# Latent attention: gate units of 256 columns placed between the heads, output projection split by input

## The chip, the cores and the metric

The kernel runs on one core of one Trainium2 chip. The metric is the device time of one execution in microseconds (us), lower being better; the time before is the median of three runs.

## What is computed

Two transformer blocks in float32 for 256 tokens of width 2048: a retention layer, a layer of latent attention, a layer of forgetting and dilated attention, and an expert lookup. The change touches the latent layer alone. Cut to what matters:

```python
def mla_branch(h, pos, w_in, q_norm_g, w_uq, kv_norm_g, w_ukv, w_out):
    cq, ckv, k_rope, g = split(h @ w_in)             # 512, 512, 64, 2048 columns
    q = (rmsnorm(cq, q_norm_g) @ w_uq)               # 16 heads of 128 + 64 (the 64 get rope)
    kv = (rmsnorm(ckv, kv_norm_g) @ w_ukv)           # 16 heads of 128 + 128
    k_rope = rope(k_rope)                            # one, shared by the heads
    o = causal_block_attention(q, k, v)              # softmax per head, 256 x 256
    return (silu(g) * o) @ w_out                     # 2048 x 2048
# and then x = x + gate * y, followed by the block's last rmsnorm
```

## The kernel before, in words

Every large product runs as three float32r matmuls (high by high, high by low, low by high; `three`, L1846 to L1848). The weights come in units of 512 KB. For each unit SP starts a DMA into a ring of eight buffers, ACT writes the rounded high part (`cast`, L696), DVE subtracts it to get the low part (`step`, L1160), and PE runs the unit's matmuls: 24 of 256 columns where the weight is the stationary operand (`unit_T`), 12 of 512 columns where the activation is (`unit_tok`). High and low parts have four buffers, so the cast of unit w+4 waits until PE has used up unit w. Each engine's order of work is written out by hand, one function per engine, and engines meet through counting semaphores; PE's `take(b)` is the wait until PSUM bank b has been read.

The latent layer goes: the two latents (CQ, CKV); the first 512 gate columns (G0), whose Silu (ACT, L847) goes straight from PSUM into `SGM`; the transposes of the normed latents ("C"); the shared key part (KRW), which is turned by a small matmul (`turn_rope`, L2061) and rotated by three DVE operations (`rotate`, L1263, L1265, L1268); the other 1536 gate columns in 24 units (G1, three groups of two banks each); and then the heads in four groups of four. A group has eight units (`lat_group`): 0 and 1 give the queries, 2 and 3 the part to be rotated, 4 and 5 the keys (copied from PSUM by DVE, L1485), 6 and 7 the values (copied by ACT, L882). Group 0 runs ahead of the heads; the units of the next group stand in the second to the fourth step of the group before, so the first step of a group, and the last group, have none. A head is four score matmuls (L2126 to L2129), a maximum on DVE (`soft`, L1280), two exponentials on ACT (`exps`, L743), a division on DVE (L1500), three transposes on PE (`flip`, L2107) and a copy on ACT (L750) one step later, and three matmuls with the values (L2139 to L2141) two steps later; DVE multiplies the result by the Silu in `SGM` (L1506). After the last head ACT and DVE split `SGM` into its high and low parts in four slabs (L902, L1516), and the output projection O2 runs: four column groups of eight units, each followed by a scaling and an addition to X on DVE (L1246, L1249).

In the heads banks 0 and 1 hold queries and then keys, 2 and 3 the rotated part and the values, 4 and 5 scores, 6 the transposes, 7 the head's output.

## Time and profile before

| what | value |
|---|---|
| median of 3 runs | 3264.48 us (3261.02 to 3265.04) |
| the profiled execution's own time | 3269.56 us |
| its span | 3267.8 us |
| PE matmul busy over the span | 2901.9 us (89%) |
| DVE busy | 2159.6 us (66%) |
| ACT busy | 1106.9 us (34%) |
| mean granted PE clock | 0.936 |
| G1's gate units, heads and O2 | from 1057 to 1367 us of the span |

The profile is one execution; its times are counted from the start of its span, which is 1.8 us shorter than the execution. A busy share is an average over stages with different limits. Matmuls are pipelined and their ends are modelled, so PE's pace is read from the distance of starts.

### The profile page before, as it was taken

How to read it: one execution, taken by the hardware profiler on the slowest of the kernel's cores; microseconds unless marked ns; L12 is line 12 of the kernel's file. 1: busy time of each engine (PE TensorE's matmuls, PEld its weight loads, DVE VectorE, ACT ScalarE, POOL GpSimd, SP SyncE). 2: the span in 40 equal slices, each digit the busy share in tenths (PEclk: the TensorE clock that was granted, in tenths of full speed). 3: DMA queues.
4: the chain of work that ended last, by engine and by line, in shares of the span. 5: the costliest groups of instructions: out<-in, count | busy, mean ns of one | idle time of the engine just before them, and what ended most of it. 6: DMA issues, size and time to landing. Idle time of an engine off the chain costs nothing.

```text
span 3267.8 us, 40653 instructions
## 1 busy us (share of the span) xinstructions
PE 2901.9 (89%) x15944; PEld 2427.8 (74%) x15944; DVE 2159.6 (66%) x3196; ACT 1106.9 (34%) x1716; POOL 665.4 (20%) x580
## 2 busy tenths in 40 slices
PE   3689999998989998899999989999997767999980
PEld 3689999996868977699888779888876656555540
DVE  6777777776765445534335556896568999666667
ACT  2133334334444444434334443111026766000000
POOL 5510000000000000000000000324432557544445
PEclk9689999998999999889989889999999898999995
DMA  8777787776866633446333343999994888999997
GB/s 292 245 235 255 249 274 260 261 256 200 289 196 168 176 108 116 149 123 187 104 97 113 122 150 117 353 314 389 407 347 148 279 287 311 393 410 410 410 398 294
DMA packets 359152, 807.95 MB, mean 247 GB/s; under 512 B 40121, under 2 KB 99777, under 8 KB 358193
## 3 DMA queue, kind: packets, MB, share of 16 engines
q1 hardware_dynamic: 284336, 497.89, 45.3%
q0 software_dynamic: 74624, 307.47, 25.5%
q8 instruction: 126, 2.06, 0.2%
q14 instruction: 66, 0.53, 0.0%
HBM read 803.16 MB, written 2.10 MB: 246 GB/s over the span
## 4 chain that ended last, share of the span: by engine, by line
PE 36%; DMA 18%; DVE 12%; POOL 5%; issue 4%; ACT 2%; DVEq 0%; ACTq 0%; POOLq 0%
PE ps L1846 10%; DMA s<-in_up_rows,s 10%; PE ps L1847 10%; PE ps L1848 10%; DMA s<-in_down_rows,s 8%; DVE s L1789 5%; POOL s L681 5%; DVE s L1811 1%; PE ps L2224 1%; DVE s L1754 1%; PE ps L2107 1%; DVE s L1757 1%; PE ps L2226 1%; DVE s L1661 1%; DVE s L1667 1%
## 5 line engine op out<-in xcount | busy, mean ns | idle before, releaser
L1846 PE MATMUL ps<-r,r 128*128 128x256 f32 (+2 forms) x3248 | 1065.1, 328 | 76.7 <-DVE r L1160 44.3
L1847 PE MATMUL ps<-r,r 128*128 128x256 f32 (+2 forms) x3248 | 1046.2, 322 | 0.0
L1848 PE MATMUL ps<-r,r 128*128 128x256 f32 (+2 forms) x3248 | 1045.0, 322 | 0.0
L1160 DVE TENSOR_TENSOR r<-s,r 128x1024 fp32r<-128x1024 f32 (+1 forms) x532 | 648.1, 1224 | 575.9 <-ACT r L696 575.7
L696 ACT CAST r<-s 128x1024 fp32r<-128x1024 f32 (+1 forms) x532 | 550.2, 1039 | 898.5 <-PE ps L1848 851.9
L1846 PEld LDWEIGHTS ps<-r,r 128*128 128x128 f32 x3248 | 641.3, 197 | 134.1 <-DVE r L1160 41.3
L1847 PEld LDWEIGHTS ps<-r,r 128*128 128x128 f32 x3248 | 641.2, 197 | 43.0 <-issue 4.6
L1848 PEld LDWEIGHTS ps<-r,r 128*128 128x128 f32 x3248 | 640.3, 197 | 41.0
L1811 DVE SCALAR_TENSOR_TENSOR s<-s,s,s 128x1152 f32<-128x1152 f32 x256 | 362.6, 1416 | 158.2 <-DMA s<-in_up_rows,s 153.5
L1789 DVE CUSTOM_DVE_ANT_0 s<-s,s 128x1152 f32<-128x1152 f32 x256 | 344.7, 1353 | 110.1 <-DMA s<-in_down_rows,s 109.7
L681 POOL DMA_INDIRECT s<-in_down_rows,s x256 | 273.7, 1069 | 578.2 <-DVE s L1789 370.1
L2342 PE MATMUL ps<-s,s 128*128 128x256 f32 x1792 | 387.2, 379 | 0.0
L2455 PE MATMUL ps<-s,big 128*128 128x448 f32 x1024 | 386.9, 541 | 0.0
L2342 PEld LDWEIGHTS ps<-s,s 128*128 128x128 f32 x1792 | 340.5, 190 | 46.0
L681 POOL DMA_INDIRECT s<-in_up_rows,s x256 | 291.5, 1139 | 246.4 <-DVE s L1811 208.8
L2455 PEld LDWEIGHTS ps<-s,big 128*128 128x128 f32 x1024 | 195.4, 191 | 190.9 <-issue 190.9
L1178 DVE SCALAR_TENSOR_TENSOR s<-s,s,s 128x512 f32<-128x512 f32 x304 | 225.6, 779 | 2.5 <-DMA s<-in_ada_w 1.1
L665 POOL DMA_DIRECT2D s<-in_final_norm_g x1 | 0.6, 618 | 1093.6 <-DVE s L1506 1093.6
L1131 ACT ACTIVATE s<-s 128x1152 f32<-128x1152 f32 x2 | 2.3, 1164 | 469.1 <-DVE s L1811 469.1
L1051 ACT COPY big<-ps 128x512 f32<-128x512 f32 x64 | 39.2, 613 | 344.6 <-PE ps L2342 344.6
L2407 PE MATMUL ps<-s,s 128*128 128x128 f32 x384 | 59.4, 303 | 56.9 <-DVE s L1779 54.6
L2407 PEld LDWEIGHTS ps<-s,s 128*128 128x128 f32 x384 | 51.9, 208 | 73.1 <-issue 54.2
(281 smaller groups left out, 2506.6 us busy)
## 6 DMA issues: line engine op xcount, KB each, us to landing
s<-in_ada_w SPq DMA_DIRECT2D x192, 512.0 KB, 5.4
s<-in_ret_w_in SPq DMA_DIRECT2D x128, 512.0 KB, 5.3
s<-in_down_blocks SPq DMA_DIRECT2D x128, 448.0 KB, 6.6
s<-in_up_blocks SPq DMA_DIRECT2D x128, 448.0 KB, 6.8
s<-in_w_in SPq DMA_DIRECT2D x96, 512.0 KB, 3.8
s<-in_ret_w_in SPq DMA_DIRECT2D x128, 256.0 KB, 4.0
s<-in_ret_w_out SPq DMA_DIRECT2D x64, 512.0 KB, 5.5
s<-in_mla_w_in SPq DMA_DIRECT2D x48, 512.0 KB, 3.7
```

The source lines that it names most:

```text
L681: g.indirect_dma_start(out=row_buf(n), out_offset=None, in_=down_rows if n < 256 else up_rows, in_offset=bass.IndirectOffsetOnAxis(ap=EI[t ...
L696: s.copy(hi_of(w), raw_of(w)).then_inc(*hi_made.to(w))
L1160: v.tensor_tensor(lo_of(w), raw_of(w), hi_of(w).bitcast(F), ALU.subtract).then_inc(*lo_made.to(w))
L1178: r = v.scalar_tensor_tensor(out=acc[h], in0=w, scalar=cact[:, k:k + 1], in1=acc[h], op0=ALU.mult, op1=ALU.add)
L1789: v.tensor_tensor_reduce(row_buf(n), row_buf(n), HNG[:, t, :], 1.0, 0.0, ALU.mult, ALU.add, HD[t][:, j:j + 1]).then_inc(*rows_used.to(n))
L1811: v.scalar_tensor_tensor(out=X[:, t, DCOL:], in0=row_buf(256 + n), scalar=HD[t][:, j:j + 1], in1=X[:, t, DCOL:], op0=ALU.mult, op1=ALU.add ...
L1846: pe.matmul(o, lh, rh, start=start, stop=False, skip_group_check=True)
L1847: pe.matmul(o, lh, rl, start=False, stop=False, skip_group_check=True)
L1848: return pe.matmul(o, ll, rh, start=False, stop=stop, skip_group_check=True)
L2342: r = pe.matmul(bank[4 + q % 4][:, j * 256:(j + 1) * 256], w[:, k, :], XNT[:, k, :], start=k == 0, stop=k == DCOL // 128 - 1)
L2407: r = pe.matmul(bank[b][:, k * 128:(k + 1) * 128], o1[:, k, :], o2[:, k, :], start=True, stop=True)
L2455: r = pe.matmul(bank[2 * t + b][:, 0:HCOL], CO[t][:, i2 // 32, i2 % 32, :], sbuf[i2 % NS][:, b * HCOL:(b + 1) * HCOL], start=i2 == 0, stop ...
```

## The change

The 24 gate units of G1 leave their place ahead of the heads. They become six pieces of 256 gate columns with four units each (`unit(mla_in, u * 512, ..., 256, 4)`: four 128-row blocks of 256 columns where a unit had two of 512), placed after the score matmuls of a head: four units in the first and two in the second head of each group. All six pieces use PSUM bank 3; ACT runs the Silu of a piece when its first unit of the next piece is due. The values move from banks 2 and 3 to banks 0 and 1. The rotation of the shared key part moves behind the first two units of group 0. Three of the four slabs are made in step 14. O2 is split by input: the 16 units that read heads 0 to 7 stand in steps 15 to 17 (`mla_units`), their column groups are scaled and added to X on their own (`mla_add`), and the other 16 follow the last slab. The weights' DMAs follow the new order.

```diff
--- before.py
+++ after.py
-        for g in range(1, 4):
-            cols512(mla_in, 1088 + g * 512)
-        for g in range(4):
-            addw(head_units(uq, g * 768, 192, 0, 128))
-            addw(head_units(uq, g * 768, 192, 128, 64), 512)
-            addw(head_units(ukv, g * 1024, 256, 0, 128))
-            addw(head_units(ukv, g * 1024, 256, 128, 128))
-        for n in range(4):
-            cols512(mla_out, n * 512)
+
+        MLA_GATES = (4, 2, 0, 0) * 4
+        lat_w, gate_w = {}, {}
+
+        def lat_units(g, ks):
+            us = (head_units(uq, g * 768, 192, 0, 128) + head_units(uq, g * 768, 192, 128, 64)
+                  + head_units(ukv, g * 1024, 256, 0, 128) + head_units(ukv, g * 1024, 256, 128, 128))
+            for k in ks:
+                lat_w[g, k] = MG + len(lat_w) + len(gate_w)
+                addw([us[k]], 512 if k in (2, 3) else 1024)
+
+        MG = 282
+        lat_units(0, range(8))
+        for i in range(16):
+            for _ in range(MLA_GATES[i]):
+                j, u = divmod(len(gate_w), 4)
+                gate_w[j, u] = MG + len(lat_w) + len(gate_w)
+                addw([unit(mla_in, u * 512, 1600 + 256 * j, 256, 4)])
+            if i % 4 and i // 4 < 3:
+                lat_units(i // 4 + 1, ((0, 1), (2, 3, 4, 5), (6, 7))[i % 4 - 1])
+        for half in range(2):
+            for n in range(4):
+                addw([unit(mla_out, u * 256, n * 512) for u in range(4 * half, 4 * half + 4)])
...
+        def mla_units(i):
+
+            return {15: range(0, 5), 16: range(5, 10), 17: range(10, 16)}.get(i, ())
...
-            def silu_gate(g):
-                w0 = G0 if g == 0 else G1 + 8 * (g - 1)
-                for u in range(8):
-                    cast(w0 + u + 4)
-                for p in range(2):
-                    s.wait_ge(*(used_up if p else first_bank).at(w0 + 7))
-                    s.activation(flat(SGM[:, 4 * g + 2 * p:4 * g + 2 * p + 2, :]), bank[GATE_BANK[g] + p],
-                                 ACT.Silu).then_inc(*lat_silu.to(2 * g + p))
-
-            silu_gate(0)
...
-            for g in range(1, 4):
-                silu_gate(g)
+
+            def silu_gate(j):
+                s.wait_ge(*used_up.at(gate_w[j, 3]))
+                s.activation(flat(SGM[:, 4 + 2 * j:6 + 2 * j, :]), bank[3], ACT.Silu).then_inc(*lat_silu.to(2 + j))
+
+            def gate_units():
+                for j in range(6):
+                    for u in range(4):
+                        if j and u == 0:
+                            silu_gate(j - 1)
+                        cast(gate_w[j, u] + 4)
+                        yield
...
                 for t in range(2):
-                    s.wait_ge(*(used_up if t else first_bank).at(w0 + 7))
-                    s.copy(VM[a][:, t, :], bank[2 + t]).then_inc(*vm_copied.to((g, t)))
+                    s.wait_ge(*(used_up if t else first_bank).at(lat_w[g, 7]))
+                    s.copy(VM[a][:, t, :], bank[t]).then_inc(*vm_copied.to((g, t)))
...
             for _ in lat_group(0):
                 pass
-            more = None
+            def slab(i):
+                s.wait_ge(*att_out.at(("M", 4 * i + 3)))
+                sl = slice(1024 * i, 1024 * i + 1024)
+                s.copy(flat(OS[0])[:, sl], flat(SGM)[:, sl]).then_inc(*slab_hi.to(("S", i)))
+
+            more, gates = None, gate_units()
             for i in range(18):
                 if i < 16:
                     exps("M", i)
+                    for _ in range(MLA_GATES[i]):
+                        next(gates)
                 if 0 <= i - 1 < 16:
                     flip_copy("M", i - 1)
                 if i % 4 == 1 and i // 4 + 1 < 4:
                     more = lat_group(i // 4 + 1)
                     next(more)
-                elif more is not None and i < 16:
+                elif i % 4 and i // 4 < 3:
                     next(more, None)
                     next(more, None)
-            for i in range(4):
-                s.wait_ge(*att_out.at(("M", 15)))
-                sl = slice(1024 * i, 1024 * i + 1024)
-                s.copy(flat(OS[0])[:, sl], flat(SGM)[:, sl]).then_inc(*slab_hi.to(("S", i)))
-            s.wait_ge(*slab_lo.at(("S", 3)))
-            project_out("O2", O2, 8)
+                if i == 14:
+                    silu_gate(5)
+                    for j in range(3):
+                        slab(j)
+                for u in mla_units(i):
+                    cast(O2 + u + 4)
+            slab(3)
+            project_out("O2", O2 + 16, 4)
...
                         v.wait_ge(*out_read.at((x, n, t)))
+                        if x == "O2":
+                            v.wait_ge(*half_added.at((x, n, t)))
                         v.tensor_tensor(xs, OT[:, t, :], xs, ALU.add).then_inc(*out_added.to((x, n, t)))
...
-            for g in range(1, 4):
-                for u in range(8):
-                    if g == 1 and u == 0:
-                        rotate("KR", 2, 1, KR, cosM, sinM, RAW, RT, None)
-                    step(G1 + 8 * (g - 1) + u)
 
             def lat_group(g):
-                w0, a = MG + 8 * g, g % 2
-                step(w0)
-                step(w0 + 1)
+                a = g % 2
+                step(lat_w[g, 0])
+                step(lat_w[g, 1])
+                if g == 0:
+                    rotate("KR", 2, 1, KR, cosM, sinM, RAW, RT, None)
...
+            def slab(i):
+                sl = slice(1024 * i, 1024 * i + 1024)
+                v.wait_ge(*slab_hi.at(("S", i)))
+                v.tensor_tensor(flat(OS[1])[:, sl], flat(SGM)[:, sl], flat(OS[0])[:, sl].bitcast(F),
+                                ALU.subtract).then_inc(*slab_lo.to(("S", i)))
+
+            def mla_add(n):
+                for t in range(2):
+                    xs, o = X[:, t, n * 512:(n + 1) * 512], at(YG + 4096 + 512 * t, 512)
+                    v.wait_ge(*(used_up if t else first_bank).at(O2 + 4 * n + 3))
+                    if n:
+                        v.wait_ge(*half_added.at(("O2", n - 1, t)))
+                    v.tensor_tensor(o, bank[2 * (n % 2) + t], GBB[:, n * 512:(n + 1) * 512], ALU.mult).then_inc(*steps.to())
+                    v.wait_ge(*steps.at())
+                    v.tensor_tensor(xs, o, xs, ALU.add).then_inc(*half_added.to(("O2", n, t)))
+
+            more, gates = None, (w for _, w in sorted(gate_w.items()))
...
+                    for _ in range(MLA_GATES[i]):
+                        step(next(gates))
...
-            for i in range(4):
-                sl = slice(1024 * i, 1024 * i + 1024)
-                v.wait_ge(*slab_hi.at(("S", i)))
-                v.tensor_tensor(flat(OS[1])[:, sl], flat(SGM)[:, sl], flat(OS[0])[:, sl].bitcast(F),
-                                ALU.subtract).then_inc(*slab_lo.to(("S", i)))
-            v.wait_ge(*slab_lo.at(("S", 3)))
-            project_out("O2", O2, 8, GBB)
+                if i == 14:
+                    for j in range(3):
+                        slab(j)
+                for u in mla_units(i):
+                    step(O2 + u)
+                    if u % 4 == 3:
+                        mla_add(u // 4)
+            slab(3)
+            project_out("O2", O2 + 16, 4, GBB)
...
-            def project_out(x, w0, units, y):
-                        unit_tok(w, u, u == units - 1, b0, y)
+                        unit_tok(w, first + u, u == units - 1, b0, y, None, first)
...
-            def silu_gate(g):
-                w0, b0 = G0 if g == 0 else G1 + 8 * (g - 1), GATE_BANK[g]
-                take(b0)
-                take(b0 + 1)
-                for u in range(8):
-                    unit_T(w0 + u, u, u == 7, b0, HT)
-                    if g == 1 and u == 0:
-                        turn_rope("KR", 2, 256, PMm, RAW)
-                for p in range(2):
-                    free[b0 + p] = lat_silu.at(2 * g + p)
...
-            silu_gate(0)
+            take(4)
+            take(5)
+            for u in range(8):
+                unit_T(G0 + u, u, u == 7, 4, HT)
+            free[4], free[5] = lat_silu.at(0), lat_silu.at(1)
             for p in range(4):
                 turn("C", p, CTOK, lambda t, k: lat_normed.at((k // 4, t)))
             take(2)
             for u in range(2):
                 unit_T(KRW + u, u, u == 1, 2, HT, nk=8, ms=1)
-            for g in range(1, 4):
-                silu_gate(g)
+
+            def gate_units():
+                for j in range(6):
+                    take(3)
+                    for u in range(4):
+                        unit_T(gate_w[j, u], u, u == 3, 3, HT, nk=4, ms=2)
+                        if u == 3:
+                            free[3] = lat_silu.at(2 + j)
+                        yield
 
...
+                if g == 0:
+                    turn_rope("KR", 2, 256, PMm, RAW)
                 free[0], free[1] = qn_copied.at((g, 0)), qn_copied.at((g, 1))
...
-                take(2)
-                take(3)
+                take(0)
+                take(1)
                 for u in range(2):
-                    unit_tok(w0 + 6 + u, u, u == 1, 2, ck)
-                free[2], free[3] = vm_copied.at((g, 0)), vm_copied.at((g, 1))
+                    unit_tok(lat_w[g, 6 + u], u, u == 1, 0, ck)
+                free[0], free[1] = vm_copied.at((g, 0)), vm_copied.at((g, 1))
                 yield
...
+                    for _ in range(MLA_GATES[i]):
+                        next(gates)
...
+                for w in mla_units(i):
+                    n, u = w // 4, w % 4
+                    b0 = 2 * (n % 2)
+                    if u == 0:
+                        take(b0)
+                        take(b0 + 1)
+                    if n == 0 and u % 2 == 0:
+                        pe.wait_ge(*slab_lo.at(("S", u // 2)))
+                    unit_tok(O2 + w, u, u == 3, b0, OS)
+                    if u == 3:
+                        for t in range(2):
+                            free[b0 + t] = half_added.at(("O2", n, t))
             pe.wait_ge(*slab_lo.at(("S", 3)))
-            project_out("O2", O2, 8, OS)
+            project_out("O2", O2 + 16, 4, OS, 4)
```

How the rows of an engine's order move (names: `r_54` the weights' parts, `r_51` and `r_56` activations' parts, `s_52` the raw weights, `ps` PSUM, `s_55` the region of `SGM`; in brackets what a row waits for).

ACT at heads 0 and 1, before:

```order
L743 ACT_TABLE_LOAD
L743 ACTIVATE s_60<-s_60 128x128 [waits maxed]
L743 ACTIVATE s_60<-s_60 128x256 [waits maxed]
L743 ACTIVATE s_60<-s_60 128x128 [waits maxed]
L743 ACTIVATE s_60<-s_60 128x256 [waits maxed]
L750 COPY s_60<-ps 128x384 [waits flipped]
L696 CAST r_54<-s_52 128x1024 [waits used_up,w6]
```

and in the changed kernel:

```order
L762 ACTIVATE s_60<-s_60 128x128 [waits maxed]
L762 ACTIVATE s_60<-s_60 128x256 [waits maxed]
L715 CAST r_54<-s_52 128x1024 [waits used_up,w6]
L715 CAST r_54<-s_52 128x1024 [waits used_up,w7]
L715 CAST r_54<-s_52 128x1024 [waits used_up,w0]
L715 CAST r_54<-s_52 128x1024 [waits used_up,w1]
L762 ACTIVATE s_60<-s_60 128x128 [waits maxed]
L762 ACTIVATE s_60<-s_60 128x256 [waits maxed]
L875 ACT_TABLE_LOAD
L875 ACTIVATE s_55<-ps 128x512 [waits used_up]
L715 CAST r_54<-s_52 128x512 [waits used_up,w2]
```

Four casts stand between the exponentials of heads 0 and 1, and a table load and the first piece's Silu (L875) behind those of head 1.

PE at head 1, in the changed kernel (before, L2126 to L2129 are followed by the transposes of head 0):

```order
L2180 MATMUL ps<-s_58 128x128 [waits lat_silu]
L2181 MATMUL ps<-s_60,s_58 128x128
L2182 MATMUL ps<-s_58 128x256
L2183 MATMUL ps<-s_60,s_58 128x256
L1899 MATMUL ps<-r_51,r_54 128x256 [waits lo_made,lat_silu]
L1900 MATMUL ps<-r_51,r_54 128x256
```

The second piece's first matmul (L1899) waits for the first piece's Silu (`lat_silu`), as the first matmul of each of the five later pieces does.

DVE in group 0, in the changed kernel:

```order
L1193 TENSOR_TENSOR r_54<-s_52,r_54 128x512 [waits hi_made] x2
L1193 TENSOR_TENSOR r_54<-s_52,r_54 128x1024 [waits hi_made,turn_lo]
L1193 TENSOR_TENSOR r_54<-s_52,r_54 128x1024 [waits hi_made]
L1298 TENSOR_TENSOR s_57<-s_57,s_60 128x256 [waits rot_copied]
L1300 TENSOR_TENSOR s_57<-ps,s_60 128x256 [waits rot_turned]
L1303 TENSOR_TENSOR s_60<-s_57 128x256 [waits dve_steps]
L1193 TENSOR_TENSOR r_54<-s_52,r_54 128x1024 [waits hi_made] x2
```

The rotation of the shared key part (L1298 to L1303) now stands behind the subtractions for units 0 and 1 of group 0 and ahead of those for units 2 and 3; before, 22 subtractions of gate units stood between it and group 0.

## Rows read from the trace of the kernel before

**Rows 1.** Stretches: length, busy time by engine (instructions), granted clock, DMA share, GB/s.

```profile
1057.00:1127.00 70.00, 69.78 (x580) 69.73 (x581) 30.69 (x29) 27.30 (x31) 0.00 (x0) 1.00 0.63 178
1183.10:1218.10 35.00, 33.11 (x214) 27.73 (x214) 18.41 (x45) 15.35 (x33) 0.00 (x0) 1.00 0.38 113
1255.10:1277.50 22.40, 14.53 (x83) 10.41 (x83) 12.33 (x39) 9.76 (x25) 0.62 (x1) 0.95 0.21 78
```

**Rows 2.** Timeline of ACT in O2: start, length, instruction, [idle before, releaser].

```profile
1288.19 1.05 ACT L696 CAST r<-s 128x1024 fp32r<-128x1024 f32 x1 [1.67 <-PE ps L1848]
```

**Rows 3.** Timeline of PE at the first scores of groups 2 and 3.

```profile
1218.16 0.46 PE L2126 MATMUL ps<-s 128*128 128x128 f32 x2 [1.89 <-issue]
...
1255.14 0.46 PE L2126 MATMUL ps<-s 128*128 128x128 f32 x2 [2.32 <-issue]
```

**Rows 4.** Timelines of ACT, PE and DVE around the shared key part.

```profile
1053.52 0.83 ACT L708 ACTIVATE s<-ps,s 128x256 f32<-128x256 f32 x2
...
1057.22 0.70 PE L2061 MATMUL ps<-s,s 128*128 128x256 f32 x2 [0.83 <-ACT s L857]
...
1058.27 0.42 DVE L1263 TENSOR_TENSOR s<-s,s 128x256 f32<-128x256 f32 x1
```

**Rows 5.** Timelines of PE (first value matmul) and DVE (key copies), groups 0 and 1.

```profile
1139.23 0.40 PE L1846 MATMUL ps<-r,r 128*128 128x512 f32 x1
...
1141.72 1.28 DVE L1485 COPY s<-ps 128x512 f32<-128x512 f32 x2
...
1175.06 1.28 DVE L1485 COPY s<-ps 128x512 f32<-128x512 f32 x2
...
1175.55 0.48 PE L1846 MATMUL ps<-r,r 128*128 128x512 f32 x1
```

**Rows 6.** Timelines at head 2: PE scores, transposes, DVE maximum, PE next unit, ACT.

```profile
1160.07 0.39 PE L2126 MATMUL ps<-s 128*128 128x128 f32 x2
...
1162.05 0.55 PE L2107 MATMUL ps<-s 128*128 128x128 f32 x3
...
1162.54 0.29 DVE L1280 CUSTOM_DVE_ANT_0 s<-ps,s 128x128 f32<-128x128 f32 x1
...
1163.03 0.37 PE L1846 MATMUL ps<-r,r 128*128 128x256 f32 x1
...
1163.76 0.46 ACT L750 COPY s<-ps 128x384 f32<-128x384 f32 x1
```

**Rows 7.** Timeline of ACT at G0's Silu.

```profile
1046.10 1.06 ACT L696 CAST r<-s 128x1024 fp32r<-128x1024 f32 x1 [1.83 <-PE ps L1848]
1047.18 1.28 ACT L847 ACT_TABLE_LOAD   x1
1048.47 1.09 ACT L847 ACTIVATE s<-ps 128x512 f32<-128x512 f32 x2
```

**Rows 8.** Timelines of ACT, DVE and PE from the last head into O2.

```profile
1271.83 3.88 ACT L902 CAST r<-s 128x1024 fp32r<-128x1024 f32 x4 [2.10 <-DVE s L1506]
...
1272.90 4.63 DVE L1516 TENSOR_TENSOR r<-s,r 128x1024 fp32r<-128x1024 f32 x4 [1.11 <-ACT r L902]
...
1277.59 0.80 PE L1846 MATMUL ps<-r,r 128*128 128x512 f32 x1 [6.26 <-DVE r L1516]
...
1304.02 0.68 DVE L1246 TENSOR_TENSOR s<-ps,s 128x512 f32<-128x512 f32 x1
```

**Rows 9.** Stretches behind PE's five idle times in the heads (columns as in rows 1).

```profile
1148.80:1155.50 6.70, 6.70 (x23) 4.94 (x23) 2.72 (x14) 2.33 (x9) 0.00 (x0) 0.51 0.00 0
1183.10:1190.00 6.90, 6.84 (x40) 5.06 (x41) 2.58 (x14) 2.65 (x10) 0.00 (x0) 1.00 0.17 38
1220.20:1224.20 4.00, 4.00 (x17) 3.02 (x16) 1.69 (x8) 1.35 (x5) 0.00 (x0) 0.57 0.13 46
1255.10:1262.00 6.90, 6.86 (x38) 4.87 (x38) 2.72 (x15) 2.66 (x10) 0.00 (x0) 1.00 0.27 97
1277.50:1282.00 4.50, 4.41 (x10) 3.47 (x11) 0.04 (x1) 0.00 (x0) 0.00 (x0) 0.50 0.00 0
```

More of the change, by code:

```diff
@@ L498, in build @@
         out_read, out_added = sig("out_read", outs[0:16]), sig("out_added", outs)
[L499 removed]
+        half_added = sig("half_added", [(x, n, t) for x in ("O2", "O3") for n in range(4) for t in range(2)])
         out_sq = sig("out_sq", outs)
@@ L839, in scalar @@
             gate_copy(1, 3)
-            def silu_gate(g):
-                w0 = G0 if g == 0 else G1 + 8 * (g - 1)
-                for u in range(8):
-                    cast(w0 + u + 4)
-                for p in range(2):
-                    s.wait_ge(*(used_up if p else first_bank).at(w0 + 7))
-                    s.activation(flat(SGM[:, 4 * g + 2 * p:4 * g + 2 * p + 2, :]), bank[GATE_BANK[g] + p],
-                                 ACT.Silu).then_inc(*lat_silu.to(2 * g + p))
-            silu_gate(0)
+            for u in range(8):
+                cast(G0 + u + 4)
+            for p in range(2):
+                s.wait_ge(*(used_up if p else first_bank).at(G0 + 7))
+                s.activation(flat(SGM[:, 2 * p:2 * p + 2, :]), bank[4 + p], ACT.Silu).then_inc(*lat_silu.to(p))
             for p in range(4):
@@ L1917, in normed, with project_out @@
                 return lambda t, k: (scaled_a if t else scaled_v).at((x, k // 4))
-            def project_out(x, w0, units, y):
+            def project_out(x, w0, units, y, first=0):
                 for n in range(4):
@@ L2062, in turn_rope @@
                 free[b] = rotated.at(key)
-            silu_gate(0)
+            take(4)
+            take(5)
+            for u in range(8):
+                unit_T(G0 + u, u, u == 7, 4, HT)
+            free[4], free[5] = lat_silu.at(0), lat_silu.at(1)
             for p in range(4):
@@ L2112, in tensor @@
                 pass
-            more = None
+            more, gates = None, gate_units()
             for i in range(18):
@@ L2258, in out_unit @@
                     for t in range(2):
-                        free[b0 + t] = out_added.at(("O3", n, t)) if u == 7 else fox_added.at((n, t))
+                        free[b0 + t] = out_added.at(("O3", n, t)) if u == 7 else half_added.at(("O3", n, t))
             for i in range(21):
```

56 lines of the change are left out of this document (27 added, 29 removed).

## The prediction

> **What bounds the kernel now.** I began with the page's busy shares (PE 89%) and its 40 slices, then cut the latent layer into stretches [rows 1]. In the gate stretch PE is busy 69.78 of 70 us at full clock, and 580 matmuls in 70 us make 24, one unit, 2.9 us. In a group of heads it is still busy 33.11 of 35 us: the heads' own matmuls and the next group's units fill it. So PE is the bound in both stretches that the change interleaves, and the 24 gate units cost their 24 x 2.9 = 69 us of PE wherever they stand. What can be won is only PE's idle time and its low clock. The timeline shows idle time at five places: before the first scores of each group, 1.89 us three times and 2.32 us once [rows 3], and from the last head to O2 [rows 8], where 7.9 of the 22.4 us of the last stretch are lost [rows 1]. Together that is 15.9 us. The wait list puts the casts on PE and SP's waits on DVE's subtraction, so weights are early and DMA (busy 0.38 to 0.63, [rows 1]) is no limit.
>
> These durations serve below. Counted from a unit's end at T (1160.07 in [rows 6]), DVE is through with that unit's subtraction and free for the next head's maximum at T + 2.47, and the exponentials end at T + 3.69, where ACT's next copy starts. A cast lasts 1.05 and a subtraction 1.16 (a quarter of 4.63 in [rows 8]), so the cast starts at about T + 0.25. A head's scores last 1.98 us, its transposes and a value product together 0.98 (1163.03 - 1162.05). An O2 unit lasts 1.05 + 1.67 = 2.72 us [rows 2].
>
> **What the change does, part by part.**
>
> *The Silu between the pieces.* All six pieces share one bank, so each but the first waits for the Silu of the piece before, and ACT comes to it in its own order. A switch from Exp to Silu costs a load of 1.28 us, and one bank of Silu half of 1.09, say 0.6 with the hand-over [rows 7].
> - Head 1: the exponentials stand ahead of the Silu. They end at T + 3.69, the load at T + 4.97, the Silu at T + 5.6 to 5.7; PE's scores end at T + 1.98. Wait: 3.7 us.
> - Head 8: the piece is long done, but its Silu stands behind head 8's exponentials. These end 1.22 us after DVE starts (1163.76 - 1162.54), 1.3 us after the scores; then 1.28 and 0.6. Wait: 3.2 us.
> - Head 9: between T and the end of the scores lie transposes and a value product, 0.98 us, but ACT must also load Exp again, 1.28 us. Wait: 3.3 us.
> - Heads 4 and 12: two pieces meet inside a step. Cast, load, Silu follow each other, as at 1046.10, 1047.18 and 1048.47 [rows 7]: 0.25 + 1.06 + 1.28 + 0.6. Wait: 3.2 us each.
>
> Sum 16.6 us. Behind the waiting piece on PE stand the transposes and values of earlier heads, so nothing else fills the time. Of the loads back to Exp only head 9's is on the path; the others lie beside gate or group units of 2.9 us each.
>
> The trace shows no idle time of ACT between the cast that ends at 1047.16, the load at 1047.18 and the Silu at 1048.47 [rows 7]. The Trainium skill, page "ScalarE: Activation LUTs", section "What ACT_TABLE_LOAD costs", adds a drain of about 1.38 us to each switch. By that rule five waits would grow by 6.9 us; I go by the rows, which speak against it here.
>
> *The shared key's rotation.* Before, it hid behind gate units, after a wait of 0.83 us [rows 4]. Now unit 0 of group 0 first waits for bank 1, which ACT's turn frees at 1053.52 + 0.83 = 1054.35 [rows 4]; the KRW units end at about 1057.22 - 0.83 - 2.9 = 1053.5, so a wait of 0.9 takes the old one's place. Then units 2 and 3 need bank 2, which the rotation frees. DVE starts it at T + 2.47 (T now the end of unit 1) and needs three operations of 0.42, so T + 3.7; PE's small matmul, 0.70 for its two halves [rows 4], covers the first 0.4. Wait: 3.3 us, with the exchange 3.4.
>
> *The values in banks 0 and 1.* They must wait until DVE has copied the keys. In group 0 the values started at 1139.23 and the copies end at 1143.0: 3.8 us more. In groups 1 to 3 a head lies between: 1176.34 against 1175.55, with the hand-over 0.85 us, three times [rows 5]: 2.5.
>
> *Scores of groups 0 to 2.* The last cast ahead of the value copies now has 1024 columns rather than 512, as already before group 3: 2.32 instead of 1.89 [rows 3]. Three times 0.43: 1.3 us.
>
> *The end.* Before, 7.9 us: 6.26 of splitting slabs [rows 8] and the rest at the last two heads. Now, in step 14, ACT does exponentials, a copy, the load, the Silu and a slab; counted from the start of that head's scores, 1.98 + 1.3 + 0.46 for the copy [rows 6], 1.28 + 0.6, then a slab copy and its subtraction, which end 2.2 us on (1.07 to the first subtraction and 1.16 for it [rows 8]): 7.8 us. PE has 2 x (1.98 + 0.98) = 5.9 us of work there. Wait: 1.9. Then 16 units run beside the last heads. After them DVE has the subtraction (T + 2.5), four operations of 0.68 for the last column group's addition [rows 8], and the last slab's subtraction, 1.2: PE waits 6.4 us. Together 8.3 against 7.9: 0.4 us lost. The other additions, three quarters of 16 extra DVE operations, lie beside units.
>
> *DMAs and queues.* As many DMAs and bytes as before, moved past each other on SP's queue alone, each still eight entries ahead; the gate weights' rows are 1 KB instead of 2 KB. I cost this at nothing, hidden by the ring; without that cover a late unit would show as a wait of ACT's cast. POOL's queue is not touched.
>
> *PE's clock.* Behind the five idle times the granted clock was 0.51 for 6.7 us, 0.57 for 4.0 and 0.50 for 4.5, and twice it stayed at 1.00 [rows 9]; 0.5 is the 1.2 GHz level. The losses are 3.3, 0, 1.7, 0 and 2.2 us, 1.45 on average. The change adds eight idle times of about 2 to 4 us (five, one, one, one); the bounds are 0 and 8 x 3.3 = 26 us. I take the average, since the new waits are as long as the old ones to within a factor of two: 11.6 us. A rule speaks against this change: the Trainium skill, "TensorE: Matmul & The Clock Gate", section "A second HAM failure mode: psum-queue depth-cycling", says that short idle times of PE between groups that cycle through PSUM make the clock go back and forth. By that rule every new wait would pay; two of five rows disagree.
>
> **Sum.** 16.6 + 3.4 + 3.8 + 2.5 + 1.3 + 0.4 = 28.0 us of waits, plus 11.6 of clock: 39.6 us. Against the profiled execution that is 3269.6 + 39.6 = 3309.2; the median of the runs lies 5.1 below that execution, so I predict 3264.5 + 39.6 = **3304 us**.
>
> **The rivals.**
> - *It fills the holes, and is faster.* If PE found gate units or O2 units ready wherever it stood idle, the 15.9 us would go: 3248.6. This decides if the Silu of a piece ran before PE asks for the next, that is ahead of the exponentials. For it: DVE and ACT are half idle [rows 1]. Against it: the written order, and PE has hardly idle time to fill. The Trainium skill, "Perfetto Trace Analysis", section "Optimization Strategy", advises to interleave regimes whose most contended engine differs; here both have the same. Chance 0.05.
> - *The bank's waits are short* because ACT runs ahead: only rotation, values, scores and the end remain, 3.4 + 3.8 + 2.5 + 1.3 + 0.4 = 11.4, less what I have overrated or with some of the clock's cost: 3270 to 3284. Chance 0.06; a third of it would read as no change.
> - *The drain of the table loads* adds 6.9: 3311. Chance 0.03.
> - *The clock stays low.* If the waits keep PE at 1.2 GHz through most gate units, half of the 69 us is lost once more, and the sum is 28 + 35 to 69: 3327 to 3361. For it: 6.7 us at 0.51 after only 1.89 us idle [rows 9]. Against it: 1.00 through whole groups [rows 1]. Chance 0.06.
>
> **Numbers.** The forecast has 0.80. Its own range is 28 less a few us of misjudged waits and no clock loss, to 28 + 26: 3284 to 3318; it takes in the third rival, and leaves out some 0.17. A measurement here can tell about 0.2%, 6.5 us. Faster 0.05, no change 0.03, slower 0.92.
>
> **What would show it.** In the changed profile: table loads at the Silu's line in the heads, and behind each an idle time of PE of 3.2 to 3.7 us that ends with ACT; an idle time of some 3.3 us that ends with the key's rotation and one of 3.8 that ends with DVE's key copy; first scores at 2.3; 1.9 and 6.4 us that end with slab subtractions. The stretch from 1057 us to the end of O2 would grow from 310 to about 350 us, and everything behind it shift unchanged. I am wrong if PE runs through the pieces without idle time, if the stretch shrinks, or if the time moves outside it.

## The result and the profile after

The changed kernel takes 3320.61 us (median of 4 runs, 3312.31 to 3321.51), the kernel before beside it 3264.76 (4 runs, 3261.02 to 3267.48): a ratio of 1.016, 95% interval 1.0147 to 1.0173. It is slower, by 52 us by that ratio and by 55.9 between the two medians, where 39.6 were forecast. The median lies 2.6 us above the upper end of the forecast's range (3318); the ratio on the 3264.48 us that the forecast started from gives 3316.7, just inside it. The profiled execution took 3320.34 us, 50.8 more than that of before. The head of its page:

```profile
span 3318.4 us, 40703 instructions
## 1 busy us (share of the span) xinstructions
PE 2929.3 (88%) x15944; PEld 2451.4 (74%) x15944; DVE 2169.9 (65%) x3212; ACT 1123.3 (34%) x1728; POOL 672.1 (20%) x580
```

PE has the same 15944 matmuls and is busy 27.4 us longer. To see where, I cut out the stretch from PE's turn of the latents ("C"), which both kernels reach with the same work behind them, to O2's last matmul. The columns are those of [rows 1]; of before:

```profile
1045.85:1366.98 321.13, 304.40 (x1884) 264.97 (x1882) 160.41 (x265) 138.64 (x225) 0.62 (x1) 0.97 0.47 142
```

and of the changed kernel:

```profile
1044.84:1414.52 369.68, 325.76 (x1884) 282.12 (x1882) 170.29 (x281) 154.69 (x237) 0.62 (x1) 0.90 0.42 125
```

The stretch grows by 48.6 us; what lies ahead of it is 1.0 us shorter, what lies behind 3.1 longer (3318.4 - 1414.52 against 3267.8 - 1366.98). The two rows split the 48.6. PE's idle time is length less busy time: 16.7 before, 43.9 after, **27.2 us of new waiting**. The busy time itself grows by **21.4 us** for the same 1884 matmuls, while the granted clock falls from 0.97 to 0.90. This split is used for every run below.

The waits, in PE's timeline of the changed kernel (all rows between them are left out, and where a kind of wait returns, some of its rows too):

```profile
1063.00 0.58 PE L1899 MATMUL ps<-r,r 128*128 128x256 f32 x1 [3.15 <-DVE s L1303]
1077.73 0.77 PE L1899 MATMUL ps<-r,r 128*128 128x512 f32 x1 [3.69 <-DVE s L1517]
1088.22 0.46 PE L2180 MATMUL ps<-s 128*128 128x128 f32 x2 [2.32 <-issue]
1109.15 0.58 PE L1899 MATMUL ps<-r,r 128*128 128x256 f32 x1 [3.69 <-ACT s L875]
1139.48 0.47 PE L1899 MATMUL ps<-r,r 128*128 128x512 f32 x1 [0.65 <-DVE s L1517]
1161.67 0.58 PE L1899 MATMUL ps<-r,r 128*128 128x256 f32 x1 [3.10 <-ACT s L875]
1215.73 0.58 PE L1899 MATMUL ps<-r,r 128*128 128x256 f32 x1 [3.32 <-ACT s L875]
1274.53 0.77 PE L2180 MATMUL ps<-s 128*128 128x128 f32 x2 [2.41 <-issue]
1315.21 0.77 PE L1899 MATMUL ps<-r,r 128*128 128x512 f32 x1 [2.05 <-DVE r L1530]
1368.57 0.79 PE L1899 MATMUL ps<-r,r 128*128 128x512 f32 x1 [6.23 <-DVE r L1530]
```

Read by the releaser: L1303 is the last operation of the shared key's rotation, L1517 DVE's key copy, L875 the Silu of a piece, L1530 the subtraction of a slab; "issue" at L2180 is a group's first scores, as in [rows 3]. The profile names no releaser there; the kernel has PE wait for ACT's copies of the values, and in group 0 the last of these ends at 1088.02, 0.20 us ahead of the scores. How a piece's wait comes about shows in ACT's timeline at head 1:

```profile
1106.61 0.49 ACT L762 ACTIVATE s<-s 128x256 f32<-128x256 f32 x1
1107.01 0.19 ACT L762 ACTIVATION_READ_ACCUMULATOR s<-s 128x1 f32 x1
1107.21 1.28 ACT L875 ACT_TABLE_LOAD   x1
1108.51 0.60 ACT L875 ACTIVATE s<-ps 128x512 f32<-128x512 f32 x1
```

PE asked for the bank at 1105.47; the exponentials, the load and the Silu end at 1109.11, and PE starts at 1109.15.

The busy time grew where the clock fell. The stretches behind the waits, with the granted clock in the third column from the right:

```profile
1063.00:1067.00 4.00, 4.00 (x22) 4.00 (x23) 0.00 (x0) 0.98 (x1) 0.00 (x0) 0.63 0.42 128
1078.30:1083.00 4.70, 4.70 (x13) 3.64 (x12) 0.00 (x0) 0.00 (x0) 0.00 (x0) 0.50 0.12 26
1088.30:1093.20 4.90, 4.90 (x20) 3.68 (x21) 1.36 (x7) 2.00 (x5) 0.00 (x0) 0.66 0.51 140
1109.50:1113.80 4.30, 4.30 (x22) 4.30 (x22) 0.00 (x0) 0.00 (x0) 0.00 (x0) 0.50 0.02 4
1139.50:1144.00 4.50, 4.50 (x20) 3.75 (x21) 1.85 (x9) 2.40 (x6) 0.00 (x0) 1.00 0.24 53
1147.50:1154.70 7.20, 7.20 (x26) 5.55 (x27) 1.42 (x8) 0.99 (x4) 0.00 (x0) 0.53 0.32 93
1162.00:1164.80 2.80, 2.80 (x14) 2.80 (x14) 0.00 (x0) 0.00 (x0) 0.00 (x0) 0.50 0.64 187
1209.00:1212.30 3.30, 3.30 (x8) 1.69 (x8) 0.00 (x1) 0.00 (x0) 0.00 (x0) 0.55 0.69 198
1216.10:1219.50 3.40, 3.40 (x17) 3.40 (x17) 0.00 (x0) 0.00 (x0) 0.00 (x0) 0.50 0.00 0
1235.80:1240.00 4.20, 4.20 (x21) 4.20 (x21) 0.00 (x0) 0.00 (x0) 0.00 (x0) 0.50 0.00 0
1274.50:1281.00 6.50, 6.47 (x21) 4.75 (x22) 1.38 (x8) 0.99 (x4) 0.00 (x0) 0.50 0.29 94
1288.90:1294.70 5.80, 5.80 (x29) 5.80 (x29) 0.00 (x0) 0.55 (x1) 0.00 (x0) 0.50 0.27 93
1315.80:1318.30 2.50, 2.50 (x7) 1.96 (x6) 1.82 (x6) 1.92 (x6) 0.00 (x0) 0.50 0.03 7
1369.10:1373.00 3.90, 3.90 (x10) 2.97 (x9) 0.00 (x0) 0.00 (x0) 0.00 (x0) 0.50 0.02 4
```

All 13 idle times of 2 us and more have a stretch behind them with a granted clock of 0.50 to 0.66; only the row at 1139.50, behind 0.65 us, stands at 1.00. Length times (1 - clock) sums to 27.1 us over those 13 rows.

### The profile page after: what moved, and what is told of

The parts are those of the page before. It is cut to its first block, busy times and chain, and to the rows that moved or that the text cites. A ratio compares the mean times of both kernels' runs of the same rounds, so it can differ in the third digit from the quotient of the medians.

```text
span 3318.4 us, 40703 instructions
## 1 busy us (share of the span) xinstructions
PE 2929.3 (88%) x15944; PEld 2451.4 (74%) x15944; DVE 2169.9 (65%) x3212; ACT 1123.3 (34%) x1728; POOL 672.1 (20%) x580
## 4 chain that ended last, share of the span: by engine, by line
PE 36%; DMA 18%; DVE 12%; POOL 4%; issue 4%; ACT 2%; DVEq 0%; ACTq 0%; POOLq 0%
PE ps L1899 10%; DMA s<-in_up_rows,s 10%; PE ps L1900 10%; PE ps L1901 10%; DMA s<-in_down_rows,s 7%; DVE s L1842 5%; POOL s L700 4%; DVE s L1864 1%; PE ps L2292 1%; DVE s L1807 1%; PE ps L1965 1%; PE ps L2294 1%; DVE s L1810 1%; DVE s L1714 1%; DVE s L1720 0%
## 5 line engine op out<-in xcount | busy, mean ns | idle before, releaser
L1899 PE MATMUL ps<-r,r 128*128 128x256 f32 (+2 forms) x3248 | 1075.3, 331 | 103.8 <-DVE r L1193 42.6
L1193 DVE TENSOR_TENSOR r<-s,r 128x1024 fp32r<-128x1024 f32 x532 | 642.7, 1214 | 618.3 <-ACT r L715 617.9
L715 ACT CAST r<-s 128x1024 fp32r<-128x1024 f32 x532 | 550.3, 1039 | 939.2 <-PE ps L1901 892.9
L1899 PEld LDWEIGHTS ps<-r,r 128*128 128x128 f32 x3248 | 649.3, 200 | 167.8 <-issue 42.8
L1900 PEld LDWEIGHTS ps<-r,r 128*128 128x128 f32 x3248 | 649.6, 200 | 43.2 <-issue 4.6
L1901 PEld LDWEIGHTS ps<-r,r 128*128 128x128 f32 x3248 | 648.4, 200 | 41.5
```

What stands on the lines that cost most here:

```text
L715: s.copy(hi_of(w), raw_of(w)).then_inc(*hi_made.to(w))
L1193: v.tensor_tensor(lo_of(w), raw_of(w), hi_of(w).bitcast(F), ALU.subtract).then_inc(*lo_made.to(w))
L1899: pe.matmul(o, lh, rh, start=start, stop=False, skip_group_check=True)
L1900: pe.matmul(o, lh, rl, start=False, stop=False, skip_group_check=True)
L1901: return pe.matmul(o, ll, rh, start=False, stop=stop, skip_group_check=True)
```

## The experiments

My theory, W: each wait of PE costs its own length and a stretch of low clock behind it, and nothing else has changed. The rivals are that gate units of four 128-row blocks (k-tiles), the order of the weights or the divided O2 cost something in themselves. The pieces are numbered from 0 to 5. Each run has its profiled execution, in which the same stretch is cut out; ratios are to the kernel before on the same chip.

| run | stretch | PE busy | idle | clock | median of the runs | ratio (95%) |
|---|---|---|---|---|---|---|
| before | 321.13 | 304.40 | 16.7 | 0.97 | | |
| the change | 369.68 | 325.76 | 43.9 | 0.90 | 3320.61 | 1.016 (1.0147 to 1.0173) |
| two banks | 344.92 | 317.77 | 27.2 | 0.94 | 3291.25 | 1.0059 (1.0042 to 1.0075) |
| O2 whole | 371.82 | 326.82 | 45.0 | 0.90 | 3319.07 | 1.0155 (1.0127 to 1.0182) |
| gates in front | 335.44 | 312.41 | 23.0 | 0.95 | 3285.85 | 1.0047 (1.003 to 1.0063) |
| dummies ahead of pieces | 362.75 | 333.77 | 29.0 | 0.93 | 3309.33 | 1.0113 (1.009 to 1.0135) |
| key and values | 355.89 | 319.05 | 36.8 | 0.92 | 3304.95 | 1.0118 (1.0101 to 1.0135) |
| last slab earlier | 360.88 | 323.38 | 37.5 | 0.91 | 3313.81 | 1.0141 (1.0123 to 1.0159) |
| dummies everywhere | 343.54 | 334.00 | 9.5 | 1.00 | 3292.59 | 1.0081 (1.0062 to 1.0101) |
| all waits | 320.39 | 307.12 | 13.3 | 0.97 | 3269.32 | 1.0006 (0.9994 to 1.0018) |
| units first | 302.88 | 298.44 | 4.4 | 0.99 | 3248.08 | 0.995 (0.9935 to 0.9964) |
| units first, O2 whole | 314.94 | 303.56 | 11.4 | 0.97 | 3263.55 | 0.9986 (0.9975 to 0.9997) |

PE busy includes the dummies where there are any. The kernel before had a median of 3271.47 us beside the first four of these edits (two banks to dummies ahead of pieces), 3266.91 beside key and values, last slab, all waits and units first, and 3267.07 beside the other two. Medians therefore differ by several us from one chip to another, and differences of a few us are read from the stretch. Where a chip is shared, the two agree to about 3 us: against O2 whole, the medians of two banks, gates in front and dummies ahead of pieces are 27.8, 33.2 and 9.7 us lower, their stretches 26.9, 36.4 and 9.1.

**Two banks.** The pieces alternate between banks 2 and 3, and a Silu stands behind a step's exponentials and casts, not in front of the next piece's first unit.

```diff
+        PIECE_BANK = (2, 3, 2, 2, 3, 2)
...
-                        if j and u == 0:
-                            silu_gate(j - 1)
...
+                    for j in {1: (0,), 5: (1, 2), 9: (3,), 12: (4,)}.get(i, ()):
+                        silu_gate(j)
...
-                    take(3)
+                    b = PIECE_BANK[j]
+                    take(b)
```

> The pieces of gate columns alternate between banks 2 and 3, and ACT runs each Silu behind the casts of a later step, so that no piece waits for a Silu. Theory (PE's waits, and the low clock behind them, are the cost): the five waits of 3.1 to 3.7 us go, 16.5 us, and the low clock behind them, some 9 us: about 25 us faster than the changed kernel, near 3295. Rival A (interleaving or the 256-column units themselves cost: their 1 KB rows, the clock under mixed work): stays within 8 us of 3320.

The five waits at L875 are gone; the idle time falls by 16.8 us (16.5 had stood at the Silu) and the busy time by 8.0. So half of the stretch's growth hung on the one bank and on where its Silu stood (the run changes both and does not part them), and the waits took clock with them.

**O2 whole.** O2 is undivided behind the heads, as before the change; only its weights' order, the slabs and the additions move back (the loop of `addw` over halves, `mla_units`, `mla_add` and the slabs in step 14 go).

> The changed kernel with the output projection undivided behind the heads, as before: four slabs, then 32 units. Theory: the end is worth little either way, 2.0 + 6.2 us of waits against 7.9, so within 4 us of 3320. Rival C (the split of the projection is what costs, by its extra additions on DVE or its place): 15 us faster or more.

The ratio is that of the change and the stretch 2.1 us longer: here the division wins next to nothing and loses nothing.

**Gates in front.** All six pieces stand ahead of the heads again, still as 24 units of 256 columns and four k-tiles.

```diff
-        MLA_GATES = (4, 2, 0, 0) * 4
+        MLA_GATES = (0,) * 16
+        for j in range(6):
+            for u in range(4):
+                gate_w[j, u] = MG + len(lat_w) + len(gate_w)
+                addw([unit(mla_in, u * 512, 1600 + 256 * j, 256, 4)])
...
-                    take(3)
+                    b = 6 + j % 2
+                    take(b)
```

> The six pieces of 256 columns stand ahead of the heads again, alternating between banks 6 and 7; all else as changed. Theory: the five Silu waits and their low clock go; left are the rotation (3.1), the values' bank (3.7 and three times 0.65) and the end (0.4), 9 us, with 2 to 6 of clock: 3274 to 3281. Rival A (the units' shape costs): stays above 3300.

PE's waits that are left, in its timeline:

```profile
1130.36 0.58 PE L1907 MATMUL ps<-r,r 128*128 128x256 f32 x1 [3.15 <-DVE s L1309]
...
1145.19 0.77 PE L1907 MATMUL ps<-r,r 128*128 128x512 f32 x1 [3.69 <-DVE s L1523]
1155.40 0.46 PE L2191 MATMUL ps<-s 128*128 128x128 f32 x2 [1.89 <-issue]
```

The units themselves run without idle time, and the first scores wait as long as before (1.89 us three times, 2.32 in group 3). The units' shape costs nothing that can be seen. The time, 3285.85 us, is above the 3274 to 3281 that I expected, on a chip where the kernel before is 7 us slower; by the ratio it would be 3280. Of the 14.3 us by which the stretch is still longer than before, 6.3 are idle time: 8.8 at the rotation and the values, less 2.5 that the kernel before had at the rotation and in the last two heads. The clock behind the rotation and group 0's values costs 4.1 us more (3.60 us at 0.56 and 5.40 at 0.53). The rest, about 3.6, is something else: the clock now falls behind all four first scores, though they wait no longer than before, where it fell behind two of four [rows 9]. The stretches behind them:

```profile
1157.00:1164.80 7.80, 7.80 (x29) 5.72 (x30) 2.73 (x14) 2.33 (x9) 0.00 (x0) 0.56 0.04 10
1194.50:1199.00 4.50, 4.50 (x18) 3.36 (x17) 1.69 (x8) 1.35 (x5) 0.00 (x0) 0.62 0.03 6
1232.00:1236.50 4.50, 4.50 (x18) 3.25 (x17) 1.70 (x8) 1.35 (x5) 0.00 (x0) 0.62 0.13 48
1269.50:1274.00 4.50, 4.50 (x18) 3.39 (x18) 1.74 (x8) 1.35 (x5) 0.00 (x0) 0.62 0.31 104
```

Length times (1 - clock) is 8.6 us here, and 5.0 in the kernel before. So the low clock behind one and the same wait differs from execution to execution.

**Dummies ahead of pieces.** Twelve matmuls of data at hand, whose result nobody reads, ahead of each of pieces 1 to 5.

```diff
+                    if j:
+                        take(2)
+                        for k in range(12):
+                            pe.matmul(bank[2], HT[0][:, k, 0:128], flat(HT[1][:, 0:2, :]), start=True, stop=True)
                     take(3)
```

> The changed kernel, with 12 matmuls of 512 columns into the unused bank 2 ahead of each of the five pieces that wait for a Silu (2.7 us at full clock, results unused): PE works in the wait, the wait itself stays. Theory (the clock falls because PE idles): the time falls by what the low clock behind these waits costs, 5 to 9 us, to 3311 to 3316. Rival B (the clock falls for another reason, so that more matmuls help nothing): the same or up to 5 us slower.

Piece after piece the bank comes free as late as in the change, but PE is busy until then, and the stretch is 6.9 us shorter although 60 matmuls were added. The time, 3309.33 us, is a little under the 3311 to 3316 expected.

**Key and values.** The rotation's matmul goes right behind unit 0, its DVE operations ahead of the subtractions, and group 0's values into banks 2 and 3.

```diff
                 for u in range(2):
                     unit_T(lat_w[g, u], u, u == 1, 0, CT, site="C" if g == 0 else None)
-                if g == 0:
-                    turn_rope("KR", 2, 256, PMm, RAW)
+                    if g == 0 and u == 0:
+                        turn_rope("KR", 2, 256, PMm, RAW)
...
-                take(0)
-                take(1)
+                b = 0 if g else 2
+                take(b)
+                take(b + 1)
```

> The shared key's rotation goes ahead again (its PE matmul right behind unit 0 of group 0, its DVE operations ahead of the two subtractions), and group 0's values go back to banks 2 and 3; everything else as in the change. Theory W (each wait costs its length and a stretch of low clock behind it): the waits of 3.14 and 3.69 us ahead of group 0's units 2 and 6 go, and with them 1.1 and 2.2 us of low clock; 7 to 11 us less than the change, a ratio to before of 1.0125 to 1.0140 in place of 1.016. Rival R (these waits are cover for something that is late anyway, the first scores of group 0 say, whose wait would grow by as much): 0 to 3 us less than the change.

The stretch loses 13.8 us, more than the 7 to 11 expected: 7.1 of idle time, as expected, and 6.7 of busy time, where the rows behind these two waits (1063.00 and 1078.30 above) have 3.8. The other 2.9 are not theirs. They lie behind two waits that this edit leaves in place, at the Silu ahead of 1276.32 and at the first slab:

```profile
1276.30:1279.50 3.20, 3.19 (x16) 3.19 (x17) 0.00 (x0) 0.00 (x0) 0.00 (x0) 0.55 0.50 169
1301.40:1305.40 4.00, 4.00 (x18) 3.31 (x19) 3.25 (x10) 3.40 (x8) 0.00 (x0) 1.00 0.00 0
```

In the change the same two places were low for longer (the rows at 1288.90 and 1315.80 above).

**Last slab earlier.** The call `slab(3)` moves from behind the loop to the head of step 17, on ACT and DVE.

> The change with one thing moved: the last slab is split at the head of step 17, ahead of that step's six O2 units on ACT and DVE. Theory W: the wait of 6.23 us ahead of the last 16 O2 units goes and 1.8 us of low clock behind it: 6 to 9 us less than the change, a ratio of 1.013 to 1.0145. Rival D: ACT and DVE then split the weights of those six units 3 to 5 us later, and PE waits for the weights instead: 0 to 3 us less than the change.

8.8 us come off the stretch: 6.4 of idle time, 2.4 of busy time. No wait for weights takes their place.

**Dummies everywhere.** The twelve of above at each piece, and more of them ahead of the rotation, the values, the first scores and both O2 waits.

> The change, with matmuls of 128 x 512 of data at hand, into a bank that nobody reads, ahead of each longer wait of PE: 11 ahead of group 0's units 2, 13 ahead of its values, 8 ahead of the first scores of each group, 12 ahead of each of pieces 1 to 5, 7 ahead of O2's first unit, 24 ahead of O2's last 16 units, 147 in all. They add work that the output does not use, and take no wait away. Theory W (the 27 us of new waiting and the 21 us by which PE's own work takes longer are two things; the second is the clock that falls because PE stands idle): the stretch from the turn of the latents to the end of O2 falls from 369.7 to 345 to 353 us, and the time to a ratio of 1.008 to 1.011. Rival P (PE's work takes longer for another reason: gate units of 4 k-tiles, half-filled banks, weights that arrive late): the stretch stays within 8 us of 369.7, or of the 362.8 of the run with dummies ahead of the pieces alone, a ratio of 1.0125 to 1.0165.

The stretch by the columns of [rows 1]:

```profile
1043.17:1386.71 343.54, 334.00 (x2031) 287.17 (x2029) 170.33 (x281) 154.60 (x237) 0.62 (x1) 1.00 0.44 134
```

and PE's timeline at the rotation, where eleven dummies stand:

```profile
1057.85 2.87 PE L2143 MATMUL ps<-r 128*128 128x512 f32 x11
1061.35 0.39 PE L1899 MATMUL ps<-r,r 128*128 128x256 f32 x1 [0.63 <-DVE s L1303]
```

This is the run that sizes the clock. No wait was taken away, 147 matmuls were added, and the stretch is 26.1 us shorter at a clock of 1.00 (1.5 us below the 345 to 353 expected). The dummies are busy 36.3 us by their own rows (14.92 ahead of the pieces, 7.90 at the scores, 5.60 + 1.87 at O2, 2.87 and 3.13 in group 0), so PE's own 1884 matmuls take about 297.7. The change's 325.76 holds 28.1 us of low clock, the 304.40 of before 6.7; the difference is the 21.4. Rival P, another reason for the longer busy time, falls.

**All waits.** Two banks (here with the Silus of pieces 4 and 5 both in step 13), key and values, and the earlier slab in one kernel.

> Three edits at once on the change: the six pieces alternate between banks 2 and 3 and their Silus stand a step or more behind them (0 in step 1, 1 and 2 in step 5, 3 in step 9, 4 and 5 in step 13); the shared key's rotation and group 0's values as in the run before this; the last slab is split at the head of step 17, ahead of that step's O2 units. Theory W: left are the first scores of the four groups, about 2.3 each, three waits of 0.65 and one of 0.9, some 12 us of waiting against 15.9 before, with a similar clock: 0 to 8 us under before, a ratio of 0.9975 to 1.0005. Rival I (interleaving itself costs, by weights that come later or by units of 4 k-tiles): 8 us or more above before, 1.0025 or more.

Interleaving without its waits costs nothing against before and wins nothing: 320.39 us against 321.13, and a ratio just above the 0.9975 to 1.0005 expected. PE saves 6.9 us of idle time from the last head into O2 (7.9 before, one wait of 1.07 now). It pays for it at the first scores (four times 2.32 us, 1.3 more than before), in three waits of 0.65 at the values, and with 2.7 us of busy time. The clock at the first scores, in two of the four stretches behind them:

```profile
1191.00:1196.40 5.40, 5.40 (x26) 5.40 (x27) 1.32 (x7) 0.99 (x4) 0.00 (x0) 0.50 0.09 26
...
1244.90:1251.00 6.10, 6.07 (x41) 5.20 (x42) 1.47 (x8) 1.77 (x5) 0.00 (x0) 1.00 0.31 107
```

**Units first.** The same kernel with a step's gate units ahead of its scores, so that they run while ACT copies the group's values.

```diff
                 if i < 16:
+                    for _ in range(MLA_GATES[i]):
+                        next(gates)
                     g, b = i // 4, 4 + i % 2
...
                     free[b] = maxed.at(("M", i, 1))
-                    for _ in range(MLA_GATES[i]):
-                        next(gates)
...
-        PIECE_BANK = (2, 3, 2, 2, 3, 2)
+        PIECE_BANK = (6, 3, 2, 2, 3, 2)
```

ACT's casts and DVE's subtractions of these units likewise go ahead of the step's exponentials and maximum, and the Silu of piece 0 moves from step 1 to step 0.

> The run before this with the gate units of a step ahead of its scores on PE, ACT and DVE (the order of the weights is the same); the first piece in bank 6 with its Silu in step 0. Theory W: PE now has 4 gate units where it waited for the first scores of a group, so those four waits of 2.3 us and the low clock behind them go as well; 8 to 16 us less than the run before this, a ratio to before of 0.993 to 0.997. Rival L: with the gate units ahead, the head's softmax is covered by fewer units, and its transposes wait for the weighing: new waits of 2 to 4 us in steps 1, 5, 9 and 13, so no gain over the run before this, or a loss of up to 8 us.

The stretch, and PE's timeline at the values of group 1, the first scores behind them and the one longer wait that is left:

```profile
1043.92:1346.80 302.88, 298.44 (x1884) 261.45 (x1882) 169.83 (x281) 149.35 (x233) 0.62 (x1) 0.99 0.50 152
```

```profile
1117.60 0.47 PE L1901 MATMUL ps<-r,r 128*128 128x512 f32 x1 [0.65 <-DVE s L1518]
...
1134.64 0.39 PE L2186 MATMUL ps<-s 128*128 128x128 f32 x2
...
1252.13 0.55 PE L2165 MATMUL ps<-s 128*128 128x128 f32 x3 [1.52 <-ACT s L770]
```

The first scores have no bracket any more: PE has no idle time in front of them. PE is busy 298.44 of 302.88 us at 0.99, and this version is faster than both kernels. On another chip it gave 3254.95 us, a ratio of 0.9954 (0.9937 to 0.9971):

> The kernel with the gate units ahead of the scores once more, so that the run before has its partner on the same chip. A ratio of 0.9935 to 0.9965, as before. If it comes out above 0.998, the gain was of the first chip alone.

The two profiled executions of this one kernel differ behind the one longer wait, 1.52 us in the first and 1.51 in the second. The stretches behind it, first and second:

```profile
1252.00:1256.50 4.50, 4.37 (x17) 3.23 (x17) 1.83 (x5) 4.47 (x9) 0.00 (x0) 0.62 0.00 0
1253.00:1261.00 8.00, 8.00 (x30) 6.04 (x31) 5.10 (x11) 6.11 (x12) 0.00 (x0) 0.57 0.01 2
```

Length times (1 - clock) is 1.7 us in one and 3.4 in the other, and the whole stretch 1.5 us longer in the second: the price of one wait in clock is not a constant, and one execution can misjudge it by this much.

**Units first, O2 whole.** The last kernel with the edit of "O2 whole" in place of the earlier slab.

> The kernel with the gate units ahead of the scores, but with O2 undivided behind the last head, as in the kernel before. Theory W: the 7.4 us of waiting and 1.8 us of low clock at the end come back: 6 to 10 us more than with the divided O2 of the next run. Rival N (the division is worth nothing, as in the run where the change alone had it undone): within 3 us of the next run.

Beside that second run of units first it is 3263.55 against 3254.95 us, 8.6 more; the stretch is 10.6 us longer than in its partner (304.38). The wait before O2 is back:

```profile
1272.54 0.79 PE L1894 MATMUL ps<-r,r 128*128 128x512 f32 x1 [6.26 <-DVE r L1527]
```

The execution profiled lies 9 us above the median of its runs, so 8.6 us is the firmer figure. So the divided O2 is worth some 9 to 11 us as soon as its last slab doesn't wait; in the change as made that wait, with its clock, ate all of it. Last slab earlier says the same: its stretch is 10.9 us shorter than that of O2 whole.

## Why the prediction was right, and where it fell short

- **Slower, by the waits named: right, at one place by luck.** Forecast 28.0 us of waiting, measured 27.2. Silu: 16.6 forecast, 16.5 measured (3.69, 3.10, 3.32, 3.32, 3.10 at heads 1, 4, 8, 9 and 12), each at its place. Rotation: 3.3 forecast, 3.15. Values: 3.8 and three times 0.85 forecast, 3.69 and three times 0.65. First scores: 2.32 as forecast, 2.41 in group 3. The end: 1.9 and 6.4 forecast, 2.05 and 6.23. The two-bank, key-and-values and last-slab runs take these waits away one kind at a time, and the idle time falls by what they were. At head 9 the 3.3 was luck: its terms do not add up to it (head 1's 3.7, less 0.98, plus a load of 1.28 would be 4.0), and the load back to Exp, which the prediction has on the path there, was not. It was over at 1232.01, and the exponentials waited on for DVE's maximum:

```profile
1230.73 1.28 ACT L762 ACT_TABLE_LOAD   x1
1232.46 0.40 ACT L762 ACTIVATE s<-s 128x128 f32<-128x128 f32 x1 [0.45 <-DVE s L1315]
```

- **DMAs at nothing: right.** No wait of PE for weights shows, and the gate units of four k-tiles ran without idle time in front of the heads.
- **The drain of the table loads: wrong, as held.** The load at 1107.21 ends at 1108.49 and the Silu starts at 1108.51; there is no place for the 1.38 us that the Trainium skill gives ("ScalarE: Activation LUTs", "What ACT_TABLE_LOAD costs").
- **The clock: the step that failed.** The prediction took "the average", eight new waits at 1.45 us, 11.6 in all; it was 21.4. By the rows of the stretches two things were missed. First, the eight new waits cost about 15.3 us (10.3 behind the Silus, 1.5, 2.4 and 1.3 behind rotation, values and the first slab): none stayed at 1.00, while the average had two zeros among five. Second, the old waits became dearer, for which the sum had no term: the four first scores, at 2.32 to 2.41 us, now lose 9.8 us of clock where [rows 9] gives 5.0. Together with the last slab (1.95 where [rows 9] gives 2.2) the rows place 19.8 of the 21.4 us. That the old waits cost more is not shown to come from the change or from their length: in gates in front they wait as long as before and lose 8.6. Both come back to a price taken from five rows of one execution, two of which were rare: of some 80 idle times of 1.88 us and more in the profiled stretches only four left the clock at 1.00, two of these in that execution. That the clock falls because PE stands idle is shown by the dummies; why these four cost nothing stays open. The rule of the Trainium skill, "TensorE: Matmul & The Clock Gate", section "A second HAM failure mode: psum-queue depth-cycling", by which, as the prediction reads it, every new wait would pay, was the better guide: the clock did fall behind all eight.
- **The base.** The execution profiled before lay 5.1 us above its median, that of the change 0.3 below; this, and not the mechanism, is a third of the 16.6 us by which 3304 fell short. The rest is 9.8 us of clock, less 0.8 of waits, and 2.1 outside the stretch.
- **Behind O2: unchanged, as far as can be told.** The 3.1 us more lie within what two executions of one kernel differ by: in units first the time behind O2's last matmul is 1899.6 us in the one and 1903.6 in the other, 1900.8 before and 1903.9 in the change. O2's norm has no part in it: over the 110 us behind O2 the mean granted clock is 0.80 both before and in the change.
- **The faster rival.** It said that if PE found units ready wherever it stood idle, the time would be 3248.6, and that the place of the Silu in ACT's order decides. The change did not do that. Units first did and took 3248.08, but the near-equality is luck: the sum had 15.9 us of idle time and no clock, while the stretch lost 12.3 of idle time and 6.0 of busy time, and on the other chip the time was 3254.95. Nor did ACT's order alone decide: all waits, with the Silus mended, won nothing until PE's units stood ahead of the scores.

## What to carry to other kernels

When PE is the bound, moved work gains only what it puts into PE's idle times: place it where PE is seen to wait, here ahead of a group's first scores, and give each accumulating piece a bank whose reader has run before the next piece asks. Price a new wait of two or more us twice, its length and the slow matmuls behind it, and take the price of the second from many waits and more than one execution: here one execution's five waits gave about half of what the change then paid. A part that "wins nothing" by itself (the divided O2) may be hidden by one late operation in its middle; look for that wait before it is thrown out.

## What the runs showed of the hardware

Matmuls that nobody needs made a kernel faster: 147 of them took 26.1 us off a stretch by holding the granted clock at 1.00. Behind idle times of 0.65 to 0.96 us it never fell in these stretches. Behind one of 1.07 us (all waits) and of 1.51 and 1.52 us (units first) it fell; behind one of 1.14 us (before) it did not. Behind those of 1.88 to 6.3 us it fell to about 0.5 nearly always, in the change for 2.5 to 7.2 us; the four exceptions are of 1.89 and 2.32 us, in before (two), key and values and all waits. The loss behind a wait was not in proportion to it: 2.0 us behind 6.23, 3.4 behind 2.32 in the change. Nor was it the same for the same wait: 1.7 and 3.4 us in two executions of units first.
